# Two output projections begun between the attention heads, and a rotation moved from TensorE to VectorE

## The reference, cut to what matters

```python
# first layer
mod = silu(c) @ w_ada + b_ada              # 6 x 1024: shift, scale, gate of attention and of ffn
h = rms_norm(x, attn_norm) * (1 + scale_a) + shift_a
... = split(h @ w_in)                      # q, kc, vc, ks, vs, kw, vw, gates, latents
q_a = rope(rms_norm(q), pos); ks, kw likewise; kc = rms_norm(compress(rope(kc)))
o_a = gated sum of compressed, selected and window attention, 8 heads of 128
o_b = latent attention, 8 heads of 128 + 64
x = x + gate_a * ((g_a * o_a + g_b * o_b) @ w_o)
x = x + gate_f * (ffn(...))                # uses shift_f, scale_f, gate_f
# second layer
gate_b, gate_c, xa, q, k, v, f = split(u @ w_in_2)
y_a = gate_b * causal_conv3(gate_c * xa)   # 512 channels
y_b = forgetting_attention(q, k, v, log_sigmoid(f))   # 8 heads of 64
m = concatenate([y_a, y_b]) @ w_out_2
```

## Time and profile before

| | |
|---|---|
| timed runs | 1167.29, 1167.33, 1169.95 us |
| profiled execution | 1167.19 us, span 1165.9 us |
| mean granted TensorE clock | 0.984 of 2.4 GHz |
| TensorE busy | 1123.2 us (96%) |
| VectorE busy | 754.2 us (65%) |
| ScalarE busy | 590.5 us (51%) |
| GpSimd busy | 46.9 us (4%) |
| DMA | 207.81 MB, mean 178 GB/s |
| chain that ended last, by engine | PE 85%, DVE 8%, ACT 3%, issue 2%, DMA 1% |

### The profile page before, as it was taken

How to read it: one execution, slowest core, us unless ns; L and a number is a source line. 1 busy time by engine, 2 the same in 40 slices (tenths; PEclk the granted TensorE clock), 3 DMA queues, 4 the chain that set the end, 5 groups by cost and what they waited for, 6 DMA issues and landing times.

```text
span 1165.9 us, 19229 instructions
## 1 busy us (share of the span) xinstructions
PE 1123.2 (96%) x7766; PEld 1020.1 (88%) x7766; DVE 754.2 (65%) x1411; ACT 590.5 (51%) x1043; POOL 46.9 (4%) x48
## 2 busy tenths in 40 slices
PE   8999998889899999999998999999999999999998
PEld 7987898789689999789987799998879978999986
DVE  3567686887677777765666666664456556666644
ACT  3365474445466666434344564444465266544542
POOL 0260000000000000101000000000000000000000
PEclk9999998999899999999998999999999999999999
DMA  8954953453135555655532465555543324555450
GB/s 323 387 196 175 377 193 131 154 208 149 69 112 200 181 183 182 252 214 180 200 109 73 161 228 186 184 184 181 183 157 131 108 97 151 205 181 181 137 188 37
DMA packets 30796, 207.81 MB, mean 178 GB/s; under 512 B 3539, under 2 KB 4051, under 8 KB 7156
## 3 DMA queue, kind: packets, MB, share of 16 engines
q1 hardware_dynamic: 30708, 206.58, 48.7%
HBM read 205.52 MB, written 1.05 MB: 177 GB/s over the span
## 4 chain that ended last, share of the span: by engine, by line
PE 85%; DVE 8%; ACT 3%; issue 2%; DMA 1%; SPq 0%; POOL 0%; ACTq 0%; DVEq 0%
PE ps L393 49%; PE ps L1645 19%; PE ps L627 3%; PE ps L411 2%; DVE wlo L352 2%; DMA raw<-wa 1%; DVE tm L566 1%; PE ps L2253 1%; PE ps L2285 1%; ACT whi L345 1%; PE ps L1343 1%; PE ps L1770 1%; PE ps L1421 1%; PE ps L816 1%; PE ps L434 1%
## 5 line engine op out<-in xcount | busy, mean ns | idle before, releaser
L352 DVE TENSOR_TENSOR wlo<-raw,whi 128x1024 fp32r<-128x1024 f32 (+2 forms) x328 | 372.0, 1176 | 251.3 <-ACT whi L345 250.8
L393 PE MATMUL ps<-H_h,whi 128*128 128x256 f32 x1552 | 446.2, 287 | 0.0
L393 PE MATMUL ps<-H_l,whi 128*128 128x256 f32 x1552 | 440.5, 284 | 0.0
L393 PE MATMUL ps<-H_h,wlo 128*128 128x256 f32 x1552 | 440.4, 284 | 0.0
L345 ACT ACTIVATE whi<-raw 128x1024 fp32r<-128x1024 f32 (+2 forms) x328 | 315.4, 1011 | 176.5 <-PE ps L1645 110.8
L393 PEld LDWEIGHTS ps<-H_h,whi 128*128 128x128 f32 x1552 | 299.3, 193 | 3.9 <-issue 3.3
L393 PEld LDWEIGHTS ps<-H_l,whi 128*128 128x128 f32 x1552 | 299.4, 193 | 0.7 <-issue 0.5
L393 PEld LDWEIGHTS ps<-H_h,wlo 128*128 128x128 f32 x1552 | 299.1, 193 | 0.0
L1645 PE MATMUL ps<-whi,gl_h 128*128 128x512 f32 x264 | 105.6, 400 | 0.5 <-DVE wlo L352 0.5
L1645 PE MATMUL ps<-whi,gl_l 128*128 128x512 f32 x264 | 104.6, 396 | 0.0
L1645 PE MATMUL ps<-wlo,gl_h 128*128 128x512 f32 x264 | 104.6, 396 | 0.0
(11 more groups left out here) (446 smaller groups left out, 1542.8 us busy)
## 6 DMA issues: line engine op xcount, KB each, us to landing
raw<-f SPq DMA_DIRECT2D x44, 1024.0 KB, 4.9
raw<-win SPq DMA_DIRECT2D x27, 1024.0 KB, 6.8
raw<-ada SPq DMA_DIRECT2D x24, 1024.0 KB, 4.9
raw<-up SPq DMA_DIRECT2D x22, 1024.0 KB, 4.8
raw<-g SPq DMA_DIRECT2D x20, 1024.0 KB, 4.8
raw<-pw SPq DMA_DIRECT2D x12, 1024.0 KB, 4.9
raw<-down SPq DMA_DIRECT2D x10, 1024.0 KB, 5.4
raw<-wa SPq DMA_DIRECT2D x4, 1024.0 KB, 10.2
```

Source lines behind the costliest of these rows:

```text
L352: dve.tensor_tensor(wlo[j % NS][:, a:b], raw_of(key)[:, a:b], whi[j % NS][:, a:b].bitcast(F32), ALU.subtract).then_inc(w_lo.hit(key, half), 1)
L393: ins_ = pe.matmul(bank[:, m * 256:(m + 1) * 256], wt[a][:, kt * w + col + m * 128:kt * w + col + m * 128 + 128], act[b][:, k0 + kt, :], s ...
```

## The change

Four things change.

1. The permutation by 64 places leaves TensorE. `head_pe2` keeps only the sum of squares, and is no longer called for kc. `rope_dve` takes the halves from the SBUF tile itself: two multiplications of 64 partitions each, crossed. The tables of sin change sign and take the plain gain, so `perm64` and three columns of parameters leave the loads.
2. TensorE's sums for `mod` and VectorE's addition of the bias come a turn later each.
3. The first unit of `w_o` is multiplied tile by tile in the turns 28 to 31 of the first attention (`ahead_pe`), into two banks of `G`; the split of its second unit moves to turn 29. `wide_pe` then skips the first unit.
4. Units 4 and 5 of `w_in_2` move to turns 3 and 5 and the short convolution's tiles to 4, 6, 7, 8. The first unit of `w_out_2` is multiplied in the turns 7, 8, 9, 9, with its rows in the order `MIXED`; the split of its second unit moves to turn 9.

```diff
-               ("cos", 256), ...   # "perm64" leaves the constants
+WO_AT, WOUT2_AT = (28, 29, 30, 31), (7, 8, 9, 9)
+MIXED = (4, 0, 5, 1, 6, 2, 3, 7)
-FOX_AT, SHORT_AT = (0, 1, 2, 4, 6), (5, 7, 8, 9)
+FOX_AT, SHORT_AT = (0, 1, 2, 3, 5), (4, 6, 7, 8)
...
 def head_pe2(pe, name):
-        pm, old = M.take(rope_b(name))
...
-        pe.matmul(pm[:], cc("perm64"), DST[name]..., start=True, stop=True).then_inc(perm_done.hit(name), 1)
-        if name != "kc":
-            sm, old = M.take(rs_ln(name))
+        sm, old = M.take(rs_ln(name))
...
 def rope_dve(...):
         dve.tensor_tensor(a, z, bc2(C, n), ALU.mult).then_inc(rope_a.hit(name), 1)
+        if zs is None:
+            dve.tensor_tensor(b[0:64], z[64:128], bc2(S_, n)[64:128], ALU.mult)
+            dve.tensor_tensor(b[64:128], z[0:64], bc2(S_, n)[0:64], ALU.mult).then_inc(rope_b.hit(name), 1)
+        else:
+            dve.wait_ge(*perm_done(name))
+            dve.tensor_tensor(b, zs, bc2(S_, n), ALU.mult).then_inc(rope_b.hit(name), 1)
...
 def attn_pe(pe):
         def ada(n):
-            if ada_ends(n - 1):
-                ada_sums_pe(pe, ada_ends(n - 1))
+            if ada_ends(n - 2):
+                ada_sums_pe(pe, ada_ends(n - 2))
+            if n in WO_AT:
+                ahead_pe(pe, "wo", H, normed("O"), WO_AT.index(n))
...
+    def wo_hi(act, n):                       # ScalarE's fill
+        if n == WO_AT[1]:
+            next_hi(act, ("wo", 0))
...
+            if n == WO_AT[1]:                # VectorE's fill
+                next_lo(dve, ("wo", 0))
-            if ada_ends(n - 2):
-                mod_dve(dve, ada_ends(n - 2))
+            if ada_ends(n - 3):
+                mod_dve(dve, ada_ends(n - 3))
...
+    def ahead_pe(pe, name, act, ready, kt, ks=range(8)):
+        key = (name, 0)
+        if kt == 0:
+            for t in range(2):
+                x, old = G.take(mt_mul(name, 0, t))
...
+        pe.wait_ge(*w_lo(key, kt // 2))
+        pe.wait_ge(*ready(ks[kt]))
+        for t in range(2):
+            for i, (a, h) in enumerate(PR):
+                ins_ = pe.matmul(where[name, 0, t][:], act[h][:, ks[kt], t * 128:(t + 1) * 128],
+                                 wt[a][:, kt * 512:(kt + 1) * 512], start=kt == 0 and i == 0, stop=False)
+        if kt == 3:
+            ins_.then_inc(unit.hit(*key), 1)
...
 def wide_pe(..., ahead=False, ks=range(NF)):
+                if ahead and cb == g == 0:
+                    k0 = nk
+                    continue
...
 def out_act / out_dve:
-            if (name, i) != ("down", 0):
+            if (name, i) not in (("down", 0), ("wo", 0), ("wout2", 0)):
...
 mix0: TensorE's, ScalarE's and VectorE's fill
+            for kt in range(4):
+                if WOUT2_AT[kt] == n:
+                    ahead_pe(pe, "wout2", yc, normed("Y"), kt, MIXED)
+            if n == WOUT2_AT[2]:
+                next_hi(act, ("wout2", 0))
+            if n == WOUT2_AT[2]:
+                next_lo(dve, ("wout2", 0))
```

More of the change, by code:

```diff
@@ L756, in head_pe2 @@
     def head_pe2(pe, name):
[L758 removed]
+        sm, old = M.take(rs_ln(name))
         if old:
             pe.wait_ge(*old)
[L761 to L770 removed]
+        where["sm", name] = sm
+        pe.wait_ge(*z_sq(name))
+        pe.matmul(sm[:], ones[:], where["zsq", name][:], start=True, stop=True).then_inc(ones_done.hit(name), 1)
     def head_act2(act, name):
@@ L948, in proj_pe @@
         pe.wait_ge(*con_in())
-        head_pe2(pe, "kc")
         head_pe2(pe, "q0")
@@ L1615, in bias_pe, with wide_pe @@
                 pe.matmul(x[:], ones[0:1, :], row[0:1, cols(cb)], start=True, stop=False)
-    def wide_pe(pe, name, act, ready, bias=False, between=None):
+    def ahead_pe(pe, name, act, ready, kt, ks=range(8)):
[3 more added lines that the diff above has]
+                x, old = G.take(mt_mul(name, 0, t))
+                if old:
+                    pe.wait_ge(*old)
+                where[name, 0, t] = x
+        j = SAT[key]
+        wt = (whi[j % NS], wlo[j % NS])
+        pe.wait_ge(*w_lo(key, kt // 2))
[6 more added lines that the diff above has]
+            ins_.then_inc(unit.hit(*key), 1)
+    def wide_pe(pe, name, act, ready, bias=False, between=None, ahead=False, ks=range(NF)):
         per = len(UNITS[name]) // 2
@@ L1621, in wide_pe @@
             for t in range(2):
-                if not bias:
+                if not bias and not (ahead and cb == 0):
                     x, old = M.take(mt_mul(name, cb, t))
@@ L2618, in _consts @@
     put("ones_hi", (p >= 64).astype(f)[:, None] * np.ones((1, 128), f))
-    for n, h in (("perm64", 64), ("perm32", 32)):
-        m = np.zeros((128, 128), f)
-        m[p ^ h, p] = 1.0
-        put(n, m)
+    m = np.zeros((128, 128), f)
+    m[p ^ 32, p] = 1.0
+    put("perm32", m)
     pos = np.arange(S, dtype=f)
@@ L2631, in _consts @@
         put(cn, co[idx])
-        put(sn, si[idx] * sign)
+        put(sn, si[idx] * (-sign if dim == 128 else sign))
     q = p[:, None]
@@ L2694, in _layout @@
     put("c", _cols(i["c"][0]))
-    for n, s in (("q_sw", "nsa_q_norm"), ("ks_sw", "nsa_ks_norm"), ("kw_sw", "nsa_kw_norm")):
-        put(n, np.roll(i[s][0], 64)[:, None])
     put("cmp_k_pe", i["cmp_k_pe"][0].T)
@@ L2758, in _layout @@
     out["wf2"] = _units(w2, k8, [np.arange(3072, 3080)])
-    out["wout2"] = _units(i["w_out_2"][0], k44, blocks(0, 2, 512))
+    out["wout2"] = _units(i["w_out_2"][0].reshape(8, 128, 1024)[list(MIXED)].reshape(1024, 1024), k44, blocks(0, 2, 512))
     for l in r(2):
```

31 lines of the change are left out of this document (14 added, 17 removed).

## The result

The changed kernel takes 1152.81 us, median of four runs (1152.02, 1152.16, 1153.45, 1155.95), against 1167.31 for the kernel before in the same comparison: a ratio of 0.988 (95% interval 0.9852 to 0.9908), 14.5 us less. Forecast were 1155.0 us. In a second comparison, on another chip, the same kernel stood at 0.9878 (0.9856 to 0.990).

What follows compares the result with a forecast made beforehand. TensorE, busy 96% of the span, was taken to bound the kernel. Terms -6.0 + 0.5 - 1.0 - 3.5 - 2.3 = -12.3 us took 1167.2 to 1154.9, stated as 1155.0, range 1149.5 to 1161.

Steps and rivals of the forecast that it cites:

- Rotation: Projections: seven permutation products of 0.86 us each leave TensorE, -6.0 us, if VectorE's splits keep up.
- ring of banks: First attention's small scores get another bank and wait for ScalarE's logarithm, +0.5 us on TensorE's path.
- splits late: Rival: VectorE's extra work delays the projections' splits, so TensorE gains less than 6.0 us; 1158.5 us, chance 10%.
- Sums for mod: First attention: a turn later TensorE no longer waits for GpSimd's addition; -1.0 us, bounds 0 and -4.2.
- w_o: End of first attention: products moved -5.7, split in the circle +3.0, clock -0.8; sum -3.5 us, range -5.2 to -1.2.
- the idle stretch is shorter but still there: Last heads of the first attention: despite the added products TensorE still waits some 2 us for the delayed job.
- a fall on six added products: w_o's clock term, upper bound: the clock falls while six added products run, +1.5 us instead of -0.8.
- slower rival: Rival: TensorE idles at the last heads and w_o's 72 remaining products run at 1.2 GHz; 1172 us, chance 4%.
- Second attention: w_out_2's second unit starts sooner, its split ahead of the table load and units earlier; -2.3 us, bounds +1 and -5.
- moving the first unit between the heads gains nothing by itself; what counts is when the second unit's split is ready: Second attention: TensorE had already done w_out_2's first unit before the second's split was ready, so only the split's time counts.
- clock stays up: Rival: three clock falls in the first attention go, 6 us more gain; 1149 us, chance 9%.
- no effect: Rival: projections' sums of squares become the pace and the permutations were hidden; about 1166 us, chance 4%.

Runs made afterwards that it cites:

- e10: Changed kernel with three split remainders subtracted by GpSimd, two high parts written in halves by ScalarE, and the ring of banks turned one place; 0.9883 of the kernel before.
- e4: Changed kernel with its whole part on w_o undone, first unit's products and second unit's split both behind the heads; 0.9931 of the kernel before.
- e5: Changed kernel with its whole part on the second attention undone: units, short convolution tiles, w_out_2's first unit and the split; 0.9915 of the kernel before.
- e6: Changed kernel with the split of w_o's second unit back behind the heads, the first unit's products still between them; 0.9930 of the kernel before.
- e13: Changed kernel with the 24 products of w_o's first unit back behind the heads, the second unit's split still at turn 29; 0.9971 of the kernel before.
- e9: Changed kernel with w_out_2's first unit and second unit's split back behind the table load, units and tiles at new turns; 0.9917 of the kernel before.
- e3: Changed kernel with the sums for mod and the bias back at their old turns; 0.9896 of the kernel before.
- e1: Kernel before with only the rotation changed, the other three parts undone; 0.9971 of the kernel before.

## Why the prediction was right, and where its steps were not

**Rotation and ring of banks: right.** Forecast -6.0 + 0.5 = -5.5; measured 110.90 to 105.23, -5.7; the ring is +0.35. The unit due at 84.5 us began at 84.46. VectorE's operations came as bounded. q0's beside GpSimd:

```profile
74.98 1.19 DVE L775 TENSOR_TENSOR tm<-q,tab_qc 128x512 f32<-128x512 f32 x1
76.20 1.07 DVE L777 TENSOR_TENSOR tm<-q,tab_qs 64x512 f32<-64x512 f32 x1
77.28 1.10 DVE L778 TENSOR_TENSOR tm<-q,tab_qs 64x512 f32<-64x512 f32 x1
...
90.63 0.69 DVE L778 TENSOR_TENSOR tm<-q,tab_qs 64x512 f32<-64x512 f32 x1
```

1.07 and 1.10 us against the 1.2 forecast, and 0.69 once GpSimd is done, which is the 0.68 taken for 64 partitions. The split between them stretched too (3.20 us), and nobody waited for it: the rival "splits late" is out. The rule of the Trainium skill, "SBUF — State Buffer", section "Who interferes with whom", that the loser blocks fully until the other has finished, agrees with e10 at the level of one instruction: 1.71 us for 0.17, ending with GpSimd's. The price is set by how long GpSimd's single instruction is.

**Sums for mod: mis-sized.** Forecast -1.0 between 0 and -4.2, measured -2.6 as a mean of profiles (2 us by the runs). The argument that VectorE's work hides the waits was right: 0.4 us of the 2.6 are not clock. What was left out is that a wait of TensorE can be paid a second time, in clock.

**w_o: right in sum, by other parts.** Forecast -5.7 + 3.0 - 0.8 = -3.5. Profile to profile it is 39.61 to 35.61, -4.0, against e4 -5.0. The split costs the 3.0: VectorE normalizes a job at 288.99 and the next, a turn of 3.2 us later, would be due at 292.2; it comes at 295.08, 2.9 late. The products bring 5.7, and the clock the rest, more than the 0.8 taken (the kernel before lost 2.8 us there, e4 4.3, the changed kernel nothing). The step "the idle stretch is shorter but still there" held (1.83 of 4 us busy), but no fall came of it in five profiles of six; the sixth, e5, paid 1.3 us, close to the +1.5 that the prediction gave for a fall on six added products. The slower rival's mechanism exists: in e6 and e13, each with one half of the part, the stretch takes 1.2 and 4.3 us longer than in the kernel before.

**Second attention: mis-sized, and one step wrong.** Forecast -2.3, measured -3.2 (79.2 against 82.4). The turns bring 1.1, the early first unit and the split ahead of the table load 2.1, where 1.3 was forecast for the table load. The step that failed is "moving the first unit between the heads gains nothing by itself; what counts is when the second unit's split is ready". With the new turns alone (e9) the split was ready 1.3 us before TensorE wanted it, so moving it ahead of the table load could gain nothing by itself. Without e9's clock fall its 96 products would start 75.6 us after the first units; the changed kernel's 72 start at 79.2. So 5.7 us leave the block, 3.6 are given back because the heads and the split end later, and 2.1 stay. What the first unit would bring with the split left behind the table load was not run.

**What was missing.** The time lost in gate unit 0 (1.7 or 3.4 us) and at the start of the second attention (0 or 3.0) is in no term. In the first profile of the changed kernel both went against it: +1.8 and +3.0. The stretches add up to -5.68 + 1.83 - 3.26 - 4.00 - 0.08 - 0.16 + 0.11 = -11.2, the difference of the spans but for 0.1; without the 3.0 they make -14.2, near the -14.5 of the medians. So the forecast of -12.3 is near both, partly by luck: terms that were too small by some 3 to 4 us stand against falls not thought of.

Of the rivals, "clock stays up" came in part: the fall at 260 us in the kernel before is gone in all profiles with the sums late and comes back in e3 (e1, with the sums early too, has one at 226 us instead), and w_o's is gone in most, but the one at gate unit 0 stayed or grew. "Splits late" did not come, and "no effect" and "slower" are excluded.

By the products of time and mean clock, 6.9 us of the gain (1148.5 to 1141.6) are work and waits at full speed, of which the rotation is 5.1; the other 7.3 (20.7 to 13.4) are time at a lower clock, idle time included.

## What to carry to other kernels

Work that fills TensorE's idle time can be worth its own length and that of the clock fall it prevents, though it did not prevent it in each profile; a filler and the operation that feeds what comes after it must move together, since here each alone gained nothing or cost. Take a change's terms from stretches of the chain cut at fixed landmarks, with the time lost to the clock beside each: in two profiles of one kernel those without a fall agreed within 0.03 us, where whole runs of it lay up to 6 apart. Several profiles are needed before a clock that stays up is called an effect of the change. An idle engine is no free help where its instruction holds up the engine on the critical circle.

## What the runs showed of the hardware that was not expected

- GpSimd's 128x1024 subtraction took 2.36 us, twice VectorE's 1.22, and held a VectorE operation on 128x2 numbers in SBUF for 1.55 us; VectorE operations on 128x255 and 128x256 numbers took 2.49 and 2.44 us beside it for 0.49 and 0.35.
- At clock 0.57, 48 products took 7.99 us after TensorE had been busy without a gap for the 2 us before and 1.38 of the 2 before those. Its only idle stretch in these 4 us was 0.6 us long. The program alone doesn't decide such a fall: the kernel before, with the same 1.38 and 2.00 us, stayed at 1.00, and the second profile of the changed kernel did too.
- VectorE's 64x512 multiplication took 0.69 us, as long as 128x512.
